# Feature stages of a two-layer decoder trunk: a unit's 512-column products ahead of its 256-column products, in place of alternating

## The reference

```python
for i in range(DEPTH):                       # DEPTH = 2
    hn = rms_norm(h, pre_mix_g[i])
    y = conformer_conv(hn, ...) if i == 0 else diff_attention(hn, ...)
    h = h + rms_norm(y, post_mix_g[i])
    f = conv_ffn(rms_norm(h, pre_ffn_g[i]), ffn_w_in[i], ffn_w_dw[i], ffn_w_out[i])
    h = h + rms_norm(f, post_ffn_g[i])
    h = h + per_layer_embed(h, p[i], ...)
# conformer_conv: x @ w_pw1 (2048 x 4096), GLU, depthwise conv of 31 taps, layer norm, silu, @ w_pw2
# diff_attention: x @ w_qkv (2048 x 6144), 8 heads of two score maps each, @ w_o
# conv_ffn:       x @ w_in (2048 x 11264), depthwise conv of 3 taps, silu(g) * up, @ w_out (5632 x 2048)
```

## Time and profile before

| | |
|---|---|
| device time, median of 3 | 2522.75 us (2521.71 to 2524.05) |
| span of the profiled execution, first to last instruction | 2521.0 us |
| mean granted clock of TensorE | 0.990 |
| TensorE busy with matmuls, with weight loads | 2450.2 us (97%), 2087.9 us (83%) |
| VectorE, ScalarE, GpSimd busy | 1666.8 us (66%), 1307.0 us (52%), 27.6 us (1%) |
| DMA | 448.28 MB, mean 178 GB/s |

### The profile page before, as it was taken

The page is one execution under the profiler, slowest core; times in us unless marked ns, Lnnn a source line. Parts: engine busy times, 40 slices in busy tenths (PEclk is TensorE's granted clock), DMA queues, the critical chain, the costliest instruction groups (busy, mean ns, idle before and its releaser), DMA issues.

```text
span 2521.0 us, 40724 instructions
## 1 busy us (share of the span) xinstructions
PE 2450.2 (97%) x12610; PEld 2087.9 (83%) x12610; DVE 1666.8 (66%) x2183; ACT 1307.0 (52%) x1882; POOL 27.6 (1%) x49
## 2 busy tenths in 40 slices
PE   7999899999999999999999999999999999999997
PEld 6888787888888888887788887888888888788876
DVE  6889766777777754446665577567777777544465
ACT  6555545555555543436454455465656666433363
POOL 1000000000000000000000000000000000000000
PEclk9999999999999999999999999999999999999999
DMA  6444264666655665555555543646666666655554
GB/s 214 134 128 136 71 195 147 195 191 188 187 185 185 199 201 186 192 189 193 179 180 183 186 151 131 203 150 189 197 191 187 189 185 185 211 189 187 188 195 139
DMA packets 365325, 448.28 MB, mean 178 GB/s; under 512 B 27084, under 2 KB 273726, under 8 KB 364076
## 3 DMA queue, kind: packets, MB, share of 16 engines
q1 hardware_dynamic: 363452, 436.75, 54.5%
q0 software_dynamic: 1776, 10.41, 1.3%
HBM read 444.95 MB, written 2.10 MB: 177 GB/s over the span
## 4 chain that ended last, share of the span: by engine, by line
PE 88%; issue 5%; DVE 3%; ACT 2%; DMA 1%; DVEq 0%; SPq 0%; POOL 0%; ACTq 0%; POOLq 0%
PE ps L1274 34%; PE ps L1276 17%; PE ps L1309 11%; PE ps L1311 11%; PE ps L1310 11%; PE ps L1347 2%; PE ps L1254 1%; DVE v_conv L936 1%; DVE w_lo L809 1%; PE ps L1413 0%; PE ps L1427 0%; DVE h L861 0%; ACT w_hi L504 0%; DMA gain<-in_post_ffn_g 0%; ACT v_conv L610 0%
## 5 line engine op out<-in xcount | busy, mean ns | idle before, releaser
L809 DVE TENSOR_TENSOR w_lo<-raw,w_hi 128x1024 fp32r<-128x1024 f32 x824 | 1002.5, 1224 | 677.7 <-ACT w_hi L504 652.2
L1274 PE MATMUL ps<-x,w_hi 128*128 128x512 f32 x3840 | 1346.5, 395 | 7.9 <-DVE w_lo L809 4.7
L504 ACT CAST w_hi<-raw 128x1024 fp32r<-128x1024 f32 x824 | 859.4, 1049 | 852.3 <-PE ps L1276 425.0
L1276 PE MATMUL ps<-x,w_lo 128*128 128x256 f32 x3840 | 1076.6, 280 | 0.0
L1274 PEld LDWEIGHTS ps<-x,w_hi 128*128 128x128 f32 x3840 | 720.7, 188 | 172.0 <-DVE w_lo L809 5.7
L1276 PEld LDWEIGHTS ps<-x,w_lo 128*128 128x128 f32 x3840 | 727.2, 189 | 0.6
L1309 PE MATMUL ps<-w_hi,mid 128*128 128x512 f32 x704 | 278.1, 395 | 3.0 <-DVE w_lo L809 3.0
L1311 PE MATMUL ps<-w_hi,mid 128*128 128x512 f32 x704 | 277.9, 395 | 0.0
L1310 PE MATMUL ps<-w_lo,mid 128*128 128x512 f32 x704 | 277.9, 395 | 0.0
L1309 PE MATMUL ps<-w_hi,x 128*128 128x512 f32 x640 | 254.9, 398 | 7.1 <-DVE x L981 3.6
L1311 PE MATMUL ps<-w_hi,x 128*128 128x512 f32 x640 | 250.8, 392 | 0.0
(11 more groups left out here) (144 smaller groups left out, 1211.9 us busy)
## 6 DMA issues: line engine op xcount, KB each, us to landing
raw<-in_ffn_w_in SPq DMA_DIRECT2D x704, 256.0 KB, 3.2
raw<-in_ffn_w_out SPq DMA_DIRECT2D x352, 256.0 KB, 3.0
raw<-in_conv_w_pw SPq DMA_DIRECT2D x192, 256.0 KB, 3.2
raw<-in_attn_w_qkv SPq DMA_DIRECT2D x192, 256.0 KB, 2.9
raw<-in_ple_w_gate SPq DMA_DIRECT2D x128, 256.0 KB, 3.4
raw<-in_attn_w_o SPq DMA_DIRECT2D x64, 256.0 KB, 3.3
raw<-in_ple_w_proj SPq DMA_DIRECT2D x16, 256.0 KB, 3.6
h<-in_x SPq DMA_DIRECT2D x4, 512.0 KB, 5.8
```

Source lines behind the costliest of these rows:

```text
L504: nc.scalar.copy(w_hi[:, u % RING], raw[:, u % RING]).then_inc(hi_split, 1)
L809: nc.vector.tensor_tensor(w_lo[:, u % RING], raw[:, u % RING], w_hi[:, u % RING].bitcast(F32), ALU.subtract).then_inc(split_done, 1)
L1274: mm(ps[:, 4 * s + f], w_hi[:, u % RING, q, columns], x[:, kt].rearrange("p a t -> p (a t)"), start=kt == 0, stop=False)
L1276: ins = mm(ps[:, 4 * s + f, 0:T], w_lo[:, u % RING, q, columns], x[:, kt, 0], start=False, stop=kt == KT - 1)
```

## The change

The loop over blocks and k-tiles inside `product` is cut in two. The first loop issues the unit's 512-column products for both k-tiles, the second its 256-column products. Operands, destinations, start and stop flags, the number of products, the waits and the increment that follows the unit's last product are as they were. Within each PSUM bank the contributions of a unit are now added in another order.

```diff
@@ -1273,6 +1273,10 @@
                             columns = slice(P * f, P * (f + 1))
                             mm(ps[:, 4 * s + f], w_hi[:, u % RING, q, columns], x[:, kt].rearrange("p a t -> p (a t)"),
                                start=kt == 0, stop=False)
+                    for q in range(UNIT_KT):
+                        kt = UNIT_KT * j + q
+                        for f in blocks:
+                            columns = slice(P * f, P * (f + 1))
                             ins = mm(ps[:, 4 * s + f, 0:T], w_lo[:, u % RING, q, columns], x[:, kt, 0],
                                      start=False, stop=kt == KT - 1)
                     return ins
```

## The result

The changed kernel takes 2527.33 us (median of 7 runs, 2522.82 to 2532.4) against 2523.21 us for the kernel before (median of 7, 2520.3 to 2524.05). The ratio is 1.002, with a 95% interval of 1.0011 to 1.003: slower by 0.2%, small but clear of zero. I had forecast no change (2522 us). The time lies inside the range, which says little, since the range is 35 us wide; the direction is that of rival B, at a fifth to a third of its price.

A forecast was written before the change was run, and what follows sets the result against it. TensorE's matmul spacing was taken as the bound. From the profiled 2521.0 us, waits, loads and streaming added 0, qk and glu -1 us, giving 2520; with 1.75 us to the median, 2522 us, range 2507 to 2542.

The forecast's parts named there:

- rival B: Feature stages: each switch of width disturbs the stream; up pays 12 to 21 us, ending at 2533 to 2544; chance 0.31.
- The bound and the waits: Whole kernel: spacing of matmuls on TensorE bounds it; waits and signals stay as before, cost 0, line 1274 some 8 us.
- Weight loads: Feature stages: sixteen loads a unit stand under the same sixteen products and fit under 256 columns; cost 0.
- Streaming: Unit of the feature stages: fixed cost per product, eight of 226.8 and eight of 119.8 are 2773 ns in either order.
- Switching: Two width switches a unit: 234 ns per long product kept as upper bound, 226.8 + 119.8 taken, so no difference.
- B's own signs: In up: a pair above 348 ns; a unit of 2.81 to 2.83 us, long products 230 to 241 ns heading runs.
- glu and qk: Taking up's pace would save 3.4 us in qk and 1.7 in glu; -1 us forecast; B: within 2 us.
- a pace is handed on: Stages without changed lines (down, v, wo, gates): forecast wrong if they move too, meaning a pace passes between stages.

The follow-up runs named there:

- Narrow: Against the changed kernel, the products with w_hi take 256 columns too, except for the first k-tile; one run, 2370.45 us.
- wide: Against the changed kernel, the products with w_lo take 512 columns too, so all feature-stage products have one width; one run, 2918.29 us.
- run 2: Not a follow-up run: the words occur only in "can run 2% apart", where run is a verb and 2% the difference in spacing.

## Why the prediction was wrong

**The bound and the waits: right.** The time is TensorE's spacing. Nothing moved across a wait, and the idle time in front of line 1274 is 8.0 us against 7.9.

**Weight loads: right.** Narrow shows sixteen and more short products in succession, each with its load, at 120 ns. The Trainium skill, page "TensorE: Matmul & The Clock Gate", section "Back-to-back issue gap", lets short products pay for their loads; at 256 columns in this format no run here does. Its formula for the gap of an isolated product, columns over 2.4 plus 2.5 ns, gives an estimate of 215.8 and 109.2 ns, where the runs have 226.7 and 120; here the measurement decides.

**Streaming: right as far as it went.** A fixed cost of 13.3 ns per product is what wide and narrow show, and steady runs of either width cost what I had taken, 226.7 and 120.

**Switching: the step that failed.** I took 226.8 + 119.8 ns "because it is the value of the longest undisturbed streams", and in the changed kernel no long run is undisturbed. The term of the sum was 0 for up; it measured 352 x 20 ns = 7 us. The row that showed it was in my hands: at the start of v the first eight long products after a short one take 234 ns each and the next nine 228. I gave it to rival B and kept the undisturbed value as my own, on the ground that up alternates at every product and is fast nevertheless. That ground does not hold: as I read it, a pattern that repeats every two products can settle and stay so, and a run of eight has to settle anew each time.

**B was oversized.** It let all eight long products pay 234 ns; they take 230.1, since they settle after five. The short ones take 119.1; the first two win 8 ns back. B's 12 to 21 us for up are 7. Rows 9 start from the slow pace of qk, which I had not allowed for: there ten products pass before 227 ns is reached. By B's own signs, the pair of 349 ns is above its 348, while the unit of 2.79 us stays below its 2.81.

**glu and qk.** I had put -1 us on them in the forecast and up to 2 us either way in B; by spacing it is -2.0 in qk and about -1 in glu. Right in sign; the new order changes width twice a unit and gives 2793 ns in every unit, so it does not stay in the slow pattern. The timed run of that part alone does not confirm it. That a stream keeps one spacing for a whole stage, as I wrote, does not hold for glu, where both occur.

**The last sentence, "a pace is handed on".** Down of layer 1 did move, from 233.3 to 232.4 ns. It does so from kernel to kernel also where the change is not near it, so a small part of the difference, 1 us, is chance of this kind.

## What to carry to other kernels

When one stream of matmuls bounds a kernel and nothing waits, read the spacing from start to start, stage by stage: the same instructions can run 2% apart. Ask of a new order how often it makes the stream change its width, and how many products it has to settle before the next change; alternation at every product can be cheaper than runs of four or eight. And before reordering anything, look at the operands' addresses: 128 bytes were worth 11 us here, the reordering -4.

## What the runs showed that I had not expected

- A stream of fp32r products settles: after a run of short products five 512-column products take 229 to 235 ns before 226.7 is reached. After qk's slow pattern, at the start of v, it is ten (241, 237, 234, 236, 224, 231, 235, 229, 232, 231). In wide nearly the same figures follow a stretch at half clock (from the starts: 258, 234, 236, 224, 231, 235, 229, 232, 231, 227).
- At half clock the fixed cost is gone. Up of layer 0 before the change, TensorE at 1.2 GHz:

```profile
403.31 0.63 PE L1274 MATMUL ps<-x,w_hi 128*128 128x512 f32 x1
403.73 0.41 PE L1276 MATMUL ps<-x,w_lo 128*128 128x256 f32 x1
403.94 0.63 PE L1274 MATMUL ps<-x,w_hi 128*128 128x512 f32 x1
```

  The starts are 0.42 and 0.21 us apart, the columns over 1.2 and nothing more.
- The start address of the stationary operand moves the steady pace of down in layer 1: 233 ns as it stood and 256 bytes higher, 229 at 64 bytes higher, 226.7 at 128 higher. The runs with 64 and 256 are one execution each.
- An alternating stream has at least two steady paces, 346.7 and 353.3 ns a pair, and holds one for 100 us and more. Which one it enters can differ between two executions of the same instructions, as in glu. What in the chip sets it stays open.
